# Splitting the normalised rows block by block in the output projection, and running the mixer's first half groups at the last norm

## The reference

```
x = x + y @ w_out[l]                  # end of the first block: "out" stage
return rms_norm(x, norm_final_g)      # x1, kept for the second residual
...
h = rmsnorm(x, norm1_w[l])            # h1
x = x + mixer(h, w_in[l], ...)        # proj = h @ w_in, 28 groups of 128 columns
h = rmsnorm(x, norm2_w[l])
x = x + hier_moe(h, ...)              # router and 64 experts
return rmsnorm(x, final_norm_w)
```

## Time and profile before

| | |
|---|---|
| median of 3 runs | 2747.14 us |
| the profiled execution's own time | 2745.43 us |
| its span, first to last instruction | 2743.6 us |
| mean granted TensorE clock | 0.930 of 2.4 GHz |
| PE busy | 2384.6 us (87%) |
| DVE / ACT / POOL busy | 774.4 / 537.9 / 571.6 us |
| out stage, PE's first to last matmul of it | 1008.27 to 1134.3 us |
| mixer, PE's first matmul to the router's first | 1153.38 to 1540.21 us |

### The profile page before, as it was taken

One profiled execution on the slowest core, in us unless ns is written; L12 is line 12 of the kernel. 1 busy time (PEld: TensorE's weight loads), 2 busy tenths in 40 slices (PEclk: granted clock), 3 DMA queues, 4 the chain that ended last, 5 costly groups with the idle time before them and its releaser, 6 DMA issues.

```text
span 2743.6 us, 42407 instructions
## 1 busy us (share of the span) xinstructions
PE 2384.6 (87%) x18656; PEld 1550.5 (57%) x18656; DVE 774.4 (28%) x1601; ACT 537.9 (20%) x1082; POOL 571.6 (21%) x374
## 2 busy tenths in 40 slices
PE   4899987788789999699999898998999898888881
PEld 4788866677567664388888555443334344434440
DVE  2311005554445533322232244111111111111114
ACT  2011123432355421211111122111101011101111
POOL 2433315323111101333233001111111111111100
PEclk9999988998889999899999998999999999999996
DMA  4122221002101001221111504899999999999994
GB/s 160 62 92 92 100 90 38 14 27 79 62 3 63 1 33 68 84 62 48 41 54 42 238 31 166 352 430 429 429 430 429 429 429 429 429 426 429 428 388 200
DMA packets 69648, 537.41 MB, mean 196 GB/s; under 512 B 13336, under 2 KB 13592, under 8 KB 43472
## 3 DMA queue, kind: packets, MB, share of 16 engines
q1 hardware_dynamic: 53152, 498.07, 43.9%
q10 hardware_dynamic: 6064, 19.71, 2.1%
q0 software_dynamic: 10240, 16.82, 1.6%
HBM read 503.08 MB, written 43.52 MB: 199 GB/s over the span
## 4 chain that ended last, share of the span: by engine, by line
PE 64%; DMA 17%; DVE 6%; issue 6%; ACT 4%; POOL 2%; ACTq 1%; POOLq 0%; SPq 0%; DVEq 0%
PE banks L219 40%; DMA arena<-in_wg 15%; PE banks L224 7%; PE banks L226 7%; PE banks L225 7%; ACT arena L229 1%; ACT arena L1519 1%; DMA arena<-in_con 1%; DMA arena<-in_fn 1%; POOL arena L1924 1%; PE banks L2681 1%; DVE arena L1498 0%; ACT arena L325 0%; DVE arena L2657 0%; DVE r L430 0%
## 5 line engine op out<-in xcount | busy, mean ns | idle before, releaser
L219 PE MATMUL banks<-arena 64*64 64x64 f32 (+14 forms) x15424 | 1706.6, 352 | 218.3 <-DMA arena<-in_wg 63.5
L219 PEld LDWEIGHTS banks<-arena 64*64 64x64 f32 (+5 forms) x15424 | 987.5, 159 | 880.0 <-issue 725.1
L229 ACT ACTIVATE arena<-banks 128x512 f32<-128x512 f32 (+6 forms) x381 | 219.8, 587 | 1478.3 <-PE banks L219 660.2
L2675 POOL DMA_INDIRECT yb<-arena x64 | 64.7, 1011 | 810.7 <-DVE arena L2786 810.7
L2786 DVE TENSOR_SCALAR arena<-banks,arena 128x512 f32<-128x512 f32 x64 | 48.1, 751 | 524.4 <-PE banks L219 524.4
L224 PE MATMUL banks<-r,w2s 128*128 128x512 f32 x448 | 177.4, 396 | 19.1 <-POOL w2s L1983 19.1
L224 PE MATMUL banks<-r,wlo 128*128 128x512 f32 x432 | 171.3, 397 | 7.2 <-POOL wlo L414 7.2
L225 PE MATMUL banks<-r,w2s 128*128 128x512 f32 x448 | 175.3, 391 | 0.0
L226 PE MATMUL banks<-r,w2s 128*128 128x512 f32 x448 | 175.1, 391 | 0.0
L226 PE MATMUL banks<-r,wlo 128*128 128x512 f32 x432 | 170.0, 394 | 0.0
L225 PE MATMUL banks<-r,wlo 128*128 128x512 f32 x432 | 169.7, 393 | 0.0
(11 more groups left out here) (242 smaller groups left out, 1521.3 us busy)
## 6 DMA issues: line engine op xcount, KB each, us to landing
arena<-in_wg SPq DMA_DIRECT2D x64, 2048.0 KB, 32.9
arena<-in_wu SPq DMA_DIRECT2D x64, 2048.0 KB, 26.6
arena<-in_wd SPq DMA_DIRECT2D x64, 2048.0 KB, 31.1
arena<-in_w SPq DMA_DIRECT2D x55, 512.0 KB, 3.2
spill<-arena SPq DMA_DIRECT2D x27, 512.0 KB, 2.6
arena<-spill SPq DMA_DIRECT2D x27, 512.0 KB, 6.0
arena<-in_wo SPq DMA_DIRECT2D x16, 512.0 KB, 7.4
arena<-in_x SPq DMA_DIRECT2D x12, 512.0 KB, 5.2
```

What stands on the lines that cost most here:

```text
L219: return pe.e.matmul(o, l, r, start=start, stop=stop)
L229: return act.e.activation(o, i, ACT.Copy)
L2675: return pool.e.indirect_dma_start(yb, bass.IndirectOffsetOnAxis(ap=six[:, col:col + 1].bitcast(U32), axis=0), src[:, :], None, bounds_che ...
```

## The change

It does five things. (1) `h1H` and `h1L` are made for each block of 128 tokens within the out stage: in `act_out` ACT copies four pieces of 128x(2x128) of the previous block, between the root of the first norm and the squares of the second; in `dve_out` and `pool_out` each engine subtracts two pieces, behind the scale of its own block. (2) Weight groups 0 and 1, and the table `rt`, are loaded at j = 2 on SP, and the groups are split by DVE and POOL at j = 5 and 6. (3) `pe_project2` does one half; the first halves of groups 0 and 1 (tokens 0 to 511) stand on PE between the transposes of blocks 6 and 7, the second halves behind those of block 7. (4) The stage's end is gone; ACT, DVE and POOL wait for the last stores of x1 at the start of the mixer in its place. (5) Tiles are laid out anew (the weight tiles and `h1H` beside `h1T`, some of the mixer's tiles where `wo` was).

```
+    def act_h1_high(act, j):
+        js = slice(j * 128, (j + 1) * 128)
+        for q in range(4):
+            u = ps["h1T", j, q // 2]
+            act.wait_ge(u.free, u.v)
+            copy(act, h1H[q][:, :, js], h1T[:, 2 * q:2 * q + 2, js]).then_inc(s("h1_high").sem, 1)
+
+    def h1_low(eng, j, half, done):
+        js = slice(j * 128, (j + 1) * 128)
+        for q in (2 * half, 2 * half + 1):
+            eng.wait_ge(s("h1_high"), 4 * j + q + 1)
+            eng.e.tensor_tensor(h1L[q][:, :, js], h1T[:, 2 * q:2 * q + 2, js], h1H[q][:, :, js].bitcast(F32),
+                                ALU.subtract).then_inc(s(done).sem, 1)
...
# sp_out
             sp.e.dma_start(xs_[j % 3][:, :], inp["x"][j * 128:(j + 1) * 128, :]).then_inc(xs_loaded(j)[0].sem, 16)
+            if j == 2:
+                sp_w2(sp, 0)
+                sp_w2(sp, 1)
+                sp.e.dma_start(rt[:, :, :], inp["rot"]).then_inc(s("rot").sem, 16)
             if j:
                 sp_store_x1(sp, j - 1)
         sp_store_x1(sp, 7)
-        for j in range(5, 8):
-            sp.wait_ge(*x1_stored(j))
...
# pe_out
+        pe_project2(pe, 0, 0)
+        pe_project2(pe, 1, 0)
         pe_turn_h1(pe, 7)
+        pe_project2(pe, 0, 1)
+        pe_project2(pe, 1, 1)
...
# dve_out, behind the scale of block j (pool_out alike, behind L1924, with half 1 and pool_w2)
+            if j:
+                h1_low(dve, j - 1, 0, "h1_low_dve")
+            if j in (5, 6):
+                dve_w2(dve, j - 5)
         dve_turn_h1(dve, 7)
+        h1_low(dve, 7, 0, "h1_low_dve")
...
# act_out
             act.e.activation(m, m, ACT.Sqrt).then_inc(s("res_root").sem, 1)
+            if j:
+                act_h1_high(act, j - 1)
             act.wait_ge(s("x1_row"), j + 1)
...
+        act_h1_high(act, 7)
...
-    end_out = stage_end(3)
+    def x1_all_stored(eng):
+        for j in range(5, 8):
+            eng.wait_ge(*x1_stored(j))
...
-    def pe_project2(pe, n):
+    def pe_project2(pe, n, x):
         wl = w2s[n % 2]
         pe.wait_ge(s("w2_low"), n + 1)
+        u = ps.open(pe, ("proj2", n, x))
+        ns = slice(x * 512, (x + 1) * 512)
+        for c in range(8):
+            pe.wait_ge(s("h1_low_pool" if c >= 4 else "h1_low_dve"), 8 * x + 8)
+            t = mm3(pe, u.t[:, :], (wl[:, 0, c, :], wl[:, 1, c, :]), (h1H[c // 2][:, c % 2, ns], h1L[c // 2][:, c % 2, ns]), c == 0, c == 7)
+        t.then_inc(u.full.sem, 1)
...
# act_mixer: the eight copies of h1T go; dve_mixer and pool_mixer: their four subtractions and group 0 (and 1) go
-        for c in range(8):
-            copy(act, h1H[c], h1T[:, c, :]).then_inc(s("h1_high").sem, 1)
+        x1_all_stored(act)
```

More of the change, by code:

```diff
@@ L1812, in program @@
     h1T = sb("h1T", [128, 8, T], c=h1s)
+    at_h1H = edge[0]
+    sb("h1H", [128, 8, T], c=h1s)
+    h1H, h1L = ([rounded(f"{n}{k}", a + 2 * k * T, 2 * T).rearrange("p (c n) -> p c n", c=2) for k in range(4)]
+                for n, a in (("h1h", at_h1H), ("h1l", at_h1T)))
+    w2r = [sb(f"w2r{i}", [128, 8, 128], c=h1s) for i in range(2)]
+    w2s = [sb(f"w2s{i}", [128, 2, 8, 128], F32R, c=h1s) for i in range(2)]
+    at_c5 = edge[0]
     c5 = Scope()
@@ L1819, in program @@
     nfg = sb("nfg", [128, D], c=c5)
-    c5.close()
+    end_c5 = edge[0]
+    rt = sb("rt", [128, 2, T], c=c5)
+    at_wo = edge[1]
     woc.close()
@@ L1924, in pool_out @@
             pool.e.tensor_scalar(hs_[j % 2][:, :], x1[j % 3][:, :], small[:, 8 + j:9 + j], None, ALU.mult).then_inc(s("h1_row").sem, 1)
-    end_out = stage_end(3)
-    c6 = Scope()
[L1930 to L1937, removed]
+            if j:
+                h1_low(pool, j - 1, 1, "h1_low_pool")
+            if j in (5, 6):
+                pool_w2(pool, j - 5)
+        h1_low(pool, 7, 1, "h1_low_pool")
+    def x1_all_stored(eng):
+        for j in range(5, 8):
+            eng.wait_ge(*x1_stored(j))
+    c6 = Scope()
+    edge[0] = at_c5
     vt = sb("vt", [128, 8, 128], c=c6)
-    gt = sb("gt", [128, T], c=c6)
     scT = sb("scT", [128, 8, 128], c=c6)
@@ L1944, in program @@
     cu = sb("cu", [128, T + 2], c=c6)
-    cg = sb("cg", [128, T], c=c6)
     ca = sb("ca", [128, T], c=c6)
     st8 = sb("st8", [128, 8], c=c6)
+    assert edge[0] <= end_c5
+    edge[0] = at_wo
+    qb, kb, qs_, ks_ = (sb(n, [128, T], c=c6) for n in ("qb", "kb", "qs_", "ks_"))
+    gt = sb("gt", [128, T], c=c6)
+    cg = sb("cg", [128, T], c=c6)
+    rc = sb("rc", [128, NRC], c=c6)
     c6.close()
+    c5.close()
     h1s.close()
@@ L1959, in w2_loaded, with sp_w2, sp_mixer @@
         return s(f"w2_slot{n % 2}"), 16 * (n // 2 + 1)
[L1961 to L1966, removed]
+    def sp_w2(sp, n):
+        if n >= 2:
+            sp.wait_ge(s("w2_low"), n - 1)
+        sp.e.dma_start(w2r[n % 2][:, :, :], inp["w2"][order2[n]]).then_inc(w2_loaded(n)[0].sem, 16)
+    def sp_mixer(sp):
+        for n in range(2, NG2):
+            sp_w2(sp, n)
     def dve_w2(dve, n):
@@ L1984, in pool_w2, with pe_projects2 @@
                                  ALU.subtract).then_inc(s("w2_low").sem, 1)
-    def pe_project2(pe, n):
+    def pe_project2(pe, n, x):
         wl = w2s[n % 2]
         pe.wait_ge(s("w2_low"), n + 1)
-        for x in range(2):
-            u = ps.open(pe, ("proj2", n, x))
-            ns = slice(x * 512, (x + 1) * 512)
-            for c in range(8):
[L1993 to L1996, removed]
+        u = ps.open(pe, ("proj2", n, x))
[4 more added lines that the diff above has]
+        t.then_inc(u.full.sem, 1)
+    def pe_projects2(pe, n):
+        if n >= 2:
+            pe_project2(pe, n, 0)
+            pe_project2(pe, n, 1)
     def to_tile(act, n, dst, func=ACT.Copy):
@@ L2014, in pe_mixer @@
             p0 = 7 * h
-            pe_project2(pe, p0)
+            pe_projects2(pe, p0)
             if h:
                 pe_ret_norm(pe, h - 1)
-            pe_project2(pe, p0 + 1)
-            pe_project2(pe, p0 + 2)
-            pe_project2(pe, p0 + 3)
+            pe_projects2(pe, p0 + 1)
+            pe_projects2(pe, p0 + 2)
+            pe_projects2(pe, p0 + 3)
             wait_tile(pe, p0 + 2)
@@ L2125, in dve_mixer @@
     def dve_mixer(dve):
+        x1_all_stored(dve)
         dve.e.memset(cu[:, 0:2], 0.0).then_inc(s("conv_zero").sem, 1)
[L2127 to L2130, removed]
         for h in range(4):
             p0 = 7 * h
-            dve_w2(dve, p0 + 1)
+            if h:
+                dve_w2(dve, p0 + 1)
             if h:
@@ L2209, in pool_mixer @@
     def pool_mixer(pool):
[L2210 to L2213, removed]
+        x1_all_stored(pool)
         for h in range(4):
             p0 = 7 * h
-            for n in range(1, 5):
+            for n in range(1 if h else 2, 5):
                 pool_w2(pool, p0 + n)
@@ L3049, in _ @@
         sp_out(sp)
-        end_out(sp)
-        sp_w2(sp)
+        sp_mixer(sp)
         sp_early(sp)
```

15 lines of the change are left out of this document (5 added, 10 removed).

## The result

Six runs of the changed kernel gave a median of 2712.04 us (2709.43 to 2720.37), six of the kernel before 2746.55 us (2742.17 to 2748.28): a ratio of 0.9883, 95% interval 0.9865 to 0.9900. That is 34.5 us by the medians, faster by more than the interval. The profiled execution of the changed kernel took 2720.37 us, 25.1 us less than the one of before. So these two numbers already disagree by 9 us on what the change is worth, and that is the question of this part.

A forecast was written before the change was run, and what follows sets the result against it. PE bounds the out stage, then idles in waits of 7.81 and 19.07 us. Waits, slow start and slow transposes go (29.4), 2.1 comes: 27.3, taken as 27.4; 2747.14 - 27.4 = 2719.7 us, range 2715 to 2726.

The forecast's parts named there:

- the scatter of a median, 1 to 2 us: Allowance within the main case of 2716 to 2721 us (chance 0.62), beside the port's 0.7 us and later slow stretches.
- The size of the gain: PE reaches the end of weight groups 0 and 1 earlier: 27.6 us by times, 27.3 by terms, 27.4 taken.
- the walk: PE's new order followed step by step from block 6's transposes (1123.50) to group 2 (1149.2, before 1176.78): 27.6 us.
- the new wait: PE behind block 7's transposes, waiting for that block's split: some 2.1 us in place of 19.07.
- its slow start: Kernel before, mixer's first eight matmuls after idle PE: 3.44 us at 0.43 each; 1.63 us to be saved.
- The clock in the new wait: Rival: the clock falls in the wait behind block 7's transposes, costing 1.6 to 3.2 us, 2721.3 to 2722.9; chance 0.21.
- DVE against POOL: Block 7's split: if DVE's second piece waits behind POOL's first, PE starts 0.7 us later (gain 26.9); otherwise 27.6, the favoured case.
- The prediction's sentence that the rows on the rounding agree with the rule: DVE's rounding, 2.76 us beside POOL against 0.69 alone, was taken to fit the skill's exclusive port lock.
- The work in the blocks at nothing: Pieces, copies and weight splits added to out-stage blocks fit idle gaps and cost nothing; uncovered, some 5 us a block.
- Group 2 late next, with 2 us to spare: Mixer: group 2's rounding and split take 3.2 us within 5.4 us of PE's work, so they fit.
- Rest of the mixer as before: From group 2 on everything stands to PE as before; 363 us to the router's first matmul.
- fall differently after a shift: Later slow clock stretches at the retention norms may land differently once shifted; named inside the main case without separate size.

The follow-up runs named there:

- experiment 8: Changed kernel with DVE and POOL swapping which half of the h1L pieces each subtracts, so both work at once in block 7; median 2715.60 us.
- Experiment 6: Changed kernel with the stage's end (barrier of all five engines) put back between out stage and mixer; median 2726.55 us, ratio 0.9931 to the kernel before.
- experiment 5: Changed kernel with block 7's transposes moved inside group 1's first half, leaving 9 matmuls behind them; median 2714.17 us, ratio 0.9896 to the kernel before.

## Why the prediction was wrong, and where it was right

- **The step that failed** is the last term of the range: "the scatter of a median, 1 to 2 us", a size for which it gave no row. Medians of the same kernel lie further apart: 2712.04, 2711.17 and 2716.11 for the changed one, 2740.82 to 2746.55 over the six sets of the kernel before, that is 4.9 and 5.7 us; single executions scatter by 3.8 to 4.6 us (standard deviation). The first three runs (2746.33 to 2748.28) agreed by luck; from them I took 2747.14 as the level of the kernel before; over 71 executions it is 2742.97. The miss of 7.7 us (2719.7 against 2712.04) is 4.2 us of this anchor, 2.9 us by which the first six executions of the changed kernel lie under the 2714.92 of all 17, and 0.6 us of gain. The 34.5 us of the result are partly luck too.
- **The size of the gain** was right: 27.6 by the walk and 27.4 as forecast; 27.7 in the first pair of profiles, 28.0 over seven, 28.1 by all medians. The walk had 25.7 us from block 6's transposes to group 2 and it took 25.54: the new wait is 1.70 us where I had 2.1 (DVE starts 0.64 us after the transposes, not 0.81, and ACT's copies are shorter), and each 48 matmuls took 11.0 us where I had 10.9. The rest is the kernel before: its slow start has 7 or 8 slow matmuls in three profiles and 14 in a fourth, where I had the 8 of one.
- **The clock in the new wait**: it stayed at full speed in all five profiles with a wait of 1.70 us, and fell in those with 2.56, 2.68 and 8.16 us (one profile each). The forecast's branch was right, with less room than I knew: at most 0.9 us.
- **DVE against POOL**: nothing of the 0.7 us came, since DVE's pieces for block 7 end (1139.55 + 0.75) as POOL's begin (1140.17). When made to overlap, they do hold each other up (experiment 8). The Trainium skill, page "SBUF — State Buffer", section "SBUF: two separate sides", says that of two such operations the one that starts first holds the shared ports for its whole instruction and that the other blocks fully. For two subtractions that fits well enough. For DVE beside POOL's scaling it does not: the pieces of block 5 (1102.47 to 1103.21) are not stretched, though the scaling begins at 1102.65. It is the scaling that becomes longer, and for these pieces. POOL's rows for blocks 0 and 1 of the changed kernel, the first with no pieces of DVE beside it, the second with two:

```profile
1030.55 2.84 POOL L1963 TENSOR_SCALAR arena<-arena 128x1024 f32<-128x1024 f32 x1 [45.02 <-DVE arena L1929]
1044.21 3.19 POOL L1963 TENSOR_SCALAR arena<-arena 128x1024 f32<-128x1024 f32 x1 [10.81 <-DVE arena L1929]
```

  It takes 3.18 or 3.19 us in each of blocks 1 to 7. The rounding stands beside it in blocks 5 and 6 alone, and there it is no longer. The rounding itself takes 1.52 us instead of 0.69 and ends at 1104.64, in the midst of the scaling. So it is slowed, but doesn't wait for the scaling's end. There the measurement decides. The prediction's sentence that the rows on the rounding agree with the rule was no test of it: the rule as told there is on operations with two inputs, and the rounding has one.
- **The work in the blocks at nothing**: right; 115.23 us from the first matmul of the out stage to block 6's transposes (the projections of all eight blocks) in all thirteen profiles, whatever was added.
- **Group 2 late next, with 2 us to spare**: right; its split on POOL ends at 1149.54, 1.9 us before PE wants it. Experiment 6 shows what happens when it is late, through the DMA that I had not thought of.
- **Rest of the mixer as before**: right for the waits, open for the clock. From group 2 to the router PE is idle for 13.6 us in all thirteen profiles. It is busy for 349.1 to 350.1 us in the four of before (mean 349.7) and for 348.9 to 354.4 in the nine with the new order (mean 351.4). The forecast named this effect ("fall differently after a shift") without a price. Whether the shift costs some 1.7 us there or these nine fell badly is open.

## What to carry to other kernels

Where a stage's last block leaves its engine idle, look for work of the next stage that needs only earlier blocks, and check that a barrier is not all that keeps it away; then check that the DMA queue gets past that barrier too. Keep back a little dense work for the short wait that remains: here 9 matmuls behind the transposes hid it (experiment 5). And before a forecast is anchored on a median of three runs, time the same code more often. A start in the timeline near the change tells the gain better than the total does: any pair of the profiles of before and changed gives 27.5 to 29.2 us for the stretch, while their total times differ by 17.3 to 36.7.

## What was not expected of the hardware

- The same 11584 matmuls up to the out stage took 999.8 to 1010.7 us in thirteen executions, while the densely filled 115.23 us behind them did not vary by 0.01. PE's idle time is nearly the same in a short and a long execution (156.9 and 155.3 us); the scatter is in its busy time, at a mean granted clock of 0.95 and 0.93.
- A wait of 1.70 us left the clock alone in five profiles; behind one of 2.56 us, at the same place, it fell.
- A DVE rounding takes 0.69 us alone, 1.52 us beside a POOL scaling, which is no longer for it, and 2.76 us beside a POOL subtraction.
- Two DVE subtractions of 0.74 us beside that scaling keep their time and lengthen it from 2.84 to 3.19 us.
